# Products with the inverse for both heads at once: all four quadrants of the array, and a second head masked across the partition halves

## The chip, the cores and the metric

The kernel runs on one core of a Trainium2 chip. The metric is the device time in microseconds (us) of one execution. TensorE (PE in the rows) does matrix products, VectorE (DVE) and ScalarE (ACT) the elementwise work, SyncE issues the DMAs.

## The reference

The program is two transformer blocks, one behind the other, on 512 tokens of width 1024. The first block has attention and a convolution; the second has an RWKV-7 time mix of 12 heads of width 64, memory attention and a feed-forward part. The change lies in the time mix, whose core is a recurrence over the tokens:

```python
def step(S, inp):
    r_t, w_t, k_t, v_t, a_t, b_t = inp
    sa = jnp.einsum('bhvk,bhk->bhv', S, a_t)
    S = (S * w_t[:, :, None, :] + sa[..., None] * b_t[:, :, None, :]
         + v_t[..., None] * k_t[:, :, None, :])
    return S, jnp.einsum('bhvk,bhk->bhv', S, r_t)
```

## The kernel before

The recurrence is computed by chunks of C = 64 tokens, eight chunks in 512 tokens, in six pairs of heads (`p` = 0 to 5, two heads `h` each). Within a chunk the state's dependence on itself is a triangular 64 x 64 system. Its matrix must be inverted for each head and chunk: 16 small inverses in a pair. Chunks go by parity `q`: those of one parity stand on partitions 0 to 63, of the other on 64 to 127 (`rows(half)`), and `c` = 0 to 3 counts the chunks of a parity. So one 128 x 256 tile holds all chunks of one head.

The inverse `X` (kept as `XN`, and its transpose as `XT`) grows by levels `b` = 2, 4, 8, 16, 32 (`LEVELS`). In each level and for each head:

1. TensorE: the product with the inverse, `times_inverse`, eight products of 64 x 64 x 64 into the PSUM bank `y{b}_{p}_{h}`. Each product is two MATMUL rows in the trace (L1310, x32 for both heads). It reads partitions `rows(1 - q)` and writes `rows(q)`, so only two of the array's four quadrants work.
2. VectorE: the mask (L2606), `Y[:, h]` = bank times the table `m{b}`. It frees the bank.
3. TensorE: `inverse_update` (L1323 and L1326, x64 for both heads), `Y` with `XT` and `XT` with `Y`, in all four quadrants. In the last level this is `last_update` (L1336, two quadrants, x32).
4. VectorE: the addition (L2641) into `XX`, which holds `XN` and `XT`.

Before, head 0's product waits for head 0's addition of the level before only, and head 1's for head 1's; the mask of head 0 can run while head 1's product does.

Each engine runs its instructions in the order in which they are written; semaphores (`is_full`, `is_free` of a bank) join them. Between these steps stands other work of the same engines. In a middle pair (1, 2, 3) TensorE has: the two halves of the next pair's `v` projection (L857 to L859) before and behind the update of level 4, `gate_low_rank` (L867) at level 8, `masked_values` (L1349) behind level 8, a sum (L1237, L1238) before the update of level 16 and another behind it, and `low_rank` (L867) at level 32 before the last update. VectorE has at level 8 the input of `v` (L2067; it waits for ScalarE's copy of the projection, L1841) ahead of the masks, and L2064 and L2481 between masks and additions; at level 16 L2539 ahead of the masks, L2510 between and L2521, L2493 behind the additions; at level 32 L2527. Pair 0 has no sum and no gate product, since there is no earlier pair. Pair 4 has no `low_rank`. Pair 5 has memory attention (L867, L1024, L1210; L2218 on VectorE) between its steps. Behind the levels come the products for the state chain, the chain itself, and the next pair.

Of the kernel before, what the change touches and what calls it, by code (L numbers as in the profile page):

```python
# [42 lines left out]
ALU = mybir.AluOpType  # L43
# [18 lines left out]
C = 64  # L62
NC = S // C
G = 4
PARITIES = 2
HEADS = 2
# [16 lines left out]
STEPS = NQ * QT  # L83
MTILES = S // P
MUNITS = 2 * MTILES
MU_AMID, MU_BEHIND = {0: 0, 1: 2, 2: 3, 4: 5}, {0: 1, 3: 4}
MU_SOLVE = len(MU_AMID) + len(MU_BEHIND)
MU_CHAIN = MU_SOLVE + 1
# [331 lines left out]
def build(nc, small, tables, xT, ctxT, memT, weights, saved, outT):  # L420
    plan = psum_plan()
    with ExitStack() as ctx:
# [89 lines left out]
        half = at  # L512
# [5 lines left out]
        NT, Y, TK, TV, MAK, MRK = (region(at + i * S, NC, C) for i in range(6)); at += 6 * S  # L518
# [8 lines left out]
        XT, XN = (heads_first(XX[:, i, :].rearrange("p (n t) -> p n t", t=C)) for i in range(2))  # L527
# [66 lines left out]
        def mask(name, *times):  # L594
            m = tab(name)
            for _ in times:
                m = m[:, None]
            return m.to_broadcast([P, *times, C])

        def rows(half):  # L600
            return slice(half * DH, (half + 1) * DH)
# [74 lines left out]
        def bank(name, w=None, rows=slice(0, P)):  # L676
            b, n = plan[name][:2]
            return psum[rows, b * S:b * S + (w or n * S)]
# [33 lines left out]
        def full_inc(ins, name):  # L712
            ins.then_inc(full[plan[name][0]], 1)

        def free_inc(ins, name):
            ins.then_inc(free[plan[name][0]], 1)
# [96 lines left out]
        def _(pe):  # L813
# [87 lines left out]
            outs = {}  # L901
# [393 lines left out]
            def key_products(name, p, x):  # L1295
                take(name)
                out = by_head(name)
                for c in range(G):
                    for q, h in QH:
                        ins = pe.matmul(out[rows(q), h, c], x[rows(h), 2 * c + q, :],  # L1300
                                        AR[p % 2][rows(h), :, 2 * c + q, :], start=True, stop=True)
                        if c == G - 1:
                            full_inc(ins, name)

            def times_inverse(name, h):

                out = take(name, G * C).rearrange("p (c t) -> p c t", c=G)
                for c in range(G):
                    for q in range(PARITIES):
                        ins = pe.matmul(out[rows(q), c, :], NT[rows(1 - q), h, c, :], XN[rows(1 - q), h, c, :],  # L1310
                                        start=True, stop=True)
                        if c == G - 1:
                            full_inc(ins, name)
# [104 lines left out]
            for p in range(NP):  # L1418
# [14 lines left out]
                for b in LEVELS:  # L1433
                    for h in range(HEADS):
                        if prev is None:
                            pe.wait_ge(x_first, p + 1)
                        else:
                            pe.wait_ge(*is_free(f"x{prev}_{p}_{h}"))
                        times_inverse(f"y{b}_{p}_{h}", h)

                    if p == NP - 1:
                        if b == LEVELS[0]:
                            gn_mean(p - 1)
                        if b == LEVELS[1]:
                            gn_square(p - 1)
                        if b == LEVELS[3]:
                            gate_low_rank(p - 1)
                        memory_unit(MU_AMID.get(LEVELS.index(b)))
                        if b == LEVELS[2]:
                            masked_values(p)  # L1450
                    else:
                        if b == LEVELS[1]:
                            project_part(f"v_{p + 1}", 0, DK // 2)
                        if p and b == LEVELS[2]:
                            gate_low_rank(p - 1)
                        if p and b == LEVELS[3]:
                            gn_square(p - 1)
                        if b == LEVELS[-1] and p + 2 < NP:
                            low_rank(p + 2)
                    for h in range(HEADS):  # L1460

                        pe.wait_ge(*is_free(f"y{b}_{p}_{h}"))
                        if b != LEVELS[-1]:
                            inverse_update(f"x{b}_{p}_{h}", h)
                        else:

                            last_update(f"xf_{p}_{h}", h)
                    if p == NP - 1:
                        memory_unit(MU_BEHIND.get(LEVELS.index(b)))
                    else:  # L1470
                        if p and b == LEVELS[0]:
                            gn_mean(p - 1)
                        if b == LEVELS[1]:
                            project_part(f"v_{p + 1}", DK // 2, DK)
                        if b == LEVELS[2]:
                            masked_values(p)
                        if b == LEVELS[3]:
                            bonus_sum(p + 1)
                        if b == LEVELS[-1]:
                            project_part(beside_chain(p, "k"), 0, 2)  # L1480
                    prev = b
# [572 lines left out]
        def _(vec):  # L2054
# [530 lines left out]
            for p in range(NP):  # L2585
# [14 lines left out]
                for b in LEVELS:  # L2600
                    if p + 1 < NP and b == LEVELS[2]:
                        pair_input(p + 1, "v")
                    for h in range(HEADS):
                        name = f"y{b}_{p}_{h}"
                        vec.wait_ge(*is_full(name))
                        free_inc(vec.tensor_tensor(Y[:, h], bank(name, G * C).rearrange("p (c t) -> p c t", c=G),  # L2606
                                                   mask(f"m{b}", G), ALU.mult), name)

                    if p == NP - 1 and b == LEVELS[0]:
                        gn_centre(p - 1)  # L2610
# [315 lines left out]
```

## Time and profile before

| | |
|---|---|
| median of 3 runs | 1069.5 us (1069.06 to 1071.4) |
| profiled execution | 1070.18 us, span 1068.4 us |
| TensorE busy | 1039.6 us, 97% |
| VectorE busy | 653.9 us, 61% |
| ScalarE busy | 453.0 us, 42% |
| granted TensorE clock | 1.0 (mean of the execution) |
| chain that ended last | TensorE 76%, VectorE 16%, ScalarE 4% |

The span is the time from the first to the last record of the profiled execution; its own time is 1.8 us longer. The chain is followed back from the last instruction to what released each one, so its shares say which engine set the time; a busy share alone does not.

### The profile page before, as it was taken

What the parts mean: (1) busy time and instruction counts of PE and PEld (TensorE: products, weight loads), DVE (VectorE), ACT (ScalarE), POOL (GpSimd) and SP (SyncE); (2) the same over time, 40 slices, a digit from 0 to 9 for tenths busy, and PEclk for the clock granted to TensorE, in tenths of its full rate; (3) what the DMA queues carried; (4) which work ended last, traced back from release to release, by engine and by line L of the source; (5) the groups of instructions that cost most, each with busy time, mean ns of one, the idle gap of its engine ahead of it and who ended that gap; (6) DMA issues with size and microseconds to landing.
All of it is one profiled execution on the core that took longest, in us unless ns stands there. A gap on an engine that the chain in (4) does not pass through costs nothing.

```text
span 1068.4 us, 22579 instructions
## 1 busy us (share of the span) xinstructions
PE 1039.6 (97%) x9816; PEld 823.4 (77%) x9816; DVE 653.9 (61%) x1025; ACT 453.0 (42%) x732; POOL 5.6 (1%) x10
## 2 busy tenths in 40 slices
PE   7999999999999989999999999999999999999998
PEld 5777777676777777777777767787888888888887
DVE  4569999977466665868677667664443223444322
ACT  5455555686335533443535245344432112443111
POOL 0000000000000000000000000000000000000000
PEclk9999999999999999999999999999999999999999
DMA  9912224000532110110110121322222232223230
GB/s 360 377 61 99 79 81 176 1 2 2 197 118 79 60 42 22 43 42 25 39 42 22 42 81 43 124 93 99 99 99 99 99 99 88 93 96 114 89 104 30
DMA packets 26161, 95.01 MB, mean 89 GB/s; under 512 B 2896, under 2 KB 3152, under 8 KB 25552
## 3 DMA queue, kind: packets, MB, share of 16 engines
q1 hardware_dynamic: 26064, 93.57, 25.1%
q8 instruction: 79, 1.29, 0.5%
q14 instruction: 18, 0.15, 0.0%
HBM read 89.36 MB, written 4.19 MB: 88 GB/s over the span
## 4 chain that ended last, share of the span: by engine, by line
PE 76%; DVE 16%; ACT 4%; issue 2%; DMA 1%; SPq 1%; POOL 0%; ACTq 0%; DVEq 0%
PE psum L857 19%; PE psum L858 18%; PE psum L859 18%; DVE work L2067 5%; PE psum L867 3%; PE psum L1310 2%; PE psum L1323 2%; DVE small_temps L2218 1%; PE psum L1045 1%; PE psum L1024 1%; PE psum L1359 1%; PE psum L1382 1%; DMA work<-weights 1%; DVE in_weights_low L2123 1%; PE psum L1110 1%
## 5 line engine op out<-in xcount | busy, mean ns | idle before, releaser
L2123 DVE TENSOR_TENSOR weights_low<-ring,weights_high 128x1024 fp32r<-128x1024 f32 x70 | 85.8, 1226 | 75.3 <-ACT weights_high L1673 75.3
L1673 ACT ACTIVATE weights_high<-ring 128x1024 fp32r<-128x1024 f32 x70 | 73.6, 1052 | 127.5 <-PE psum L859 127.5
L857 PE MATMUL psum<-normed_high,weights_high 128*128 128x512 f32 x256 | 100.2, 391 | 0.2 <-DVE weights_low L2123 0.2
L859 PE MATMUL psum<-normed_high,weights_low 128*128 128x512 f32 x256 | 99.7, 389 | 0.0
L859 PE MATMUL psum<-hidden_high,weights_low 128*128 128x512 f32 x256 | 99.7, 389 | 0.0
L858 PE MATMUL psum<-normed_low,weights_high 128*128 128x512 f32 x256 | 99.6, 389 | 0.0
L858 PE MATMUL psum<-hidden_low,weights_high 128*128 128x512 f32 x256 | 99.6, 389 | 0.0
L857 PE MATMUL psum<-hidden_high,weights_high 128*128 128x512 f32 x256 | 99.6, 389 | 0.0
L2067 DVE SCALAR_TENSOR_TENSOR work<-work,small_sb 128x512 f32<-128x512 f32 x116 | 80.2, 745 | 0.2
L1643 ACT ACTIVATE work<-psum 128x384 f32<-128x384 f32 (+1 forms) x110 | 54.1, 541 | 56.3 <-PE psum L1359 18.8
L857 PE MATMUL psum<-pair_normed_high,pair_weights_high 128*128 128x512 f32 x176 | 75.8, 431 | 0.8 <-DVE normed_low L2127 0.8
L858 PE MATMUL psum<-normed_low,pair_weights_high 128*128 128x512 f32 x176 | 69.3, 394 | 0.0
L859 PE MATMUL psum<-pair_normed_high,pair_weights_low 128*128 128x512 f32 x176 | 68.9, 392 | 0.0
L2046 ACT ACTIVATE work<-work 128x512 f32<-128x512 f32 x32 | 20.2, 632 | 100.9 <-DVE work L2064 100.9
L857 PE MATMUL psum<-normed_high,in_weights_high 128*128 128x512 f32 x144 | 59.2, 411 | 1.9 <-DVE in_weights_low L2123 1.6
L857 PEld LDWEIGHTS psum<-normed_high,weights_high 128*128 128x128 f32 x256 | 48.1, 188 | 10.8 <-issue 0.9
L859 PE MATMUL psum<-normed_high,in_weights_low 128*128 128x512 f32 x144 | 56.2, 390 | 0.0
L858 PE MATMUL psum<-normed_low,in_weights_high 128*128 128x512 f32 x144 | 56.2, 390 | 0.0
L859 PEld LDWEIGHTS psum<-normed_high,weights_low 128*128 128x128 f32 x256 | 48.1, 188 | 10.1
L858 PEld LDWEIGHTS psum<-normed_low,weights_high 128*128 128x128 f32 x256 | 48.1, 188 | 10.1 <-issue 0.2
L859 PEld LDWEIGHTS psum<-hidden_high,weights_low 128*128 128x128 f32 x256 | 48.1, 188 | 10.0
L857 PEld LDWEIGHTS psum<-hidden_high,weights_high 128*128 128x128 f32 x256 | 48.1, 188 | 9.9
(320 smaller groups left out, 2102.6 us busy)
## 6 DMA issues: line engine op xcount, KB each, us to landing
ring<-weights SPq DMA_DIRECT2D x135, 512.0 KB, 3.7
work<-weights SPq DMA_DIRECT2D x10, 512.0 KB, 12.9
residual<-xT SPq DMA_DIRECT2D x4, 512.0 KB, 7.1
mixed<-weights SPq DMA_DIRECT2D x4, 512.0 KB, 7.8
residual_saved<-residual SPq DMA_DIRECT2D x8, 256.0 KB, 4.4
residual<-residual_saved SPq DMA_DIRECT2D x1, 2048.0 KB, 9.0
outT<-residual SPq DMA_DIRECT2D x8, 256.0 KB, 3.3
tables_sb<-tables SPq DMA_DIRECT2D x1, 1280.0 KB, 10.4
```

The lines of the kernel that those rows point to most:

```text
L857: pe.matmul(out, wh, high(k), start=first and n == 0, stop=False)
L858: pe.matmul(out, wh, low(k), start=False, stop=False)
L859: ins = pe.matmul(out, wl, high(k), start=False, stop=last and n == len(order) - 1)
L867: full_inc(pe.matmul(take(name, w), stationary, moving, start=True, stop=True), name)
L1024: last = pe.transpose(out[:, t * P:(t + 1) * P], src[:, t * P:(t + 1) * P], tab("ident"))
L1310: ins = pe.matmul(out[rows(q), c, :], NT[rows(1 - q), h, c, :], XN[rows(1 - q), h, c, :], start=True, stop=True)
L1323: ins = pe.matmul(out[rows(q), 0, c, :], Y[rows(q), h, c, :], XT[rows(q), h, c, :], start=True, stop=True)
L1643: free_inc(act.activation(out, bank(name, w) if src is None else src, ACT.Copy), name)
L1673: act.activation(wsplit(q)[0], room_of(b), ACT.Copy).then_inc(w_high, 1)
L2046: act.activation(FS[:, t, :], FS[:, t, :], ACT.Square).then_inc(h_relu, 1)
L2067: return vec.scalar_tensor_tensor(out=out, in0=a, scalar=scalar, in1=b, op0=op, op1=ALU.add)
L2123: vec.tensor_tensor(low, room_of(b), high.bitcast(F32), ALU.subtract).then_inc(w_low, 1)
```

## The change

`times_inverse_both` replaces the two calls of `times_inverse` at the levels 4, 8, 16 and 32 (`CROSSED`); level 2 stays. It interleaves the heads and sends head 1's products to the other half of the partitions (`rows(q ^ h)`), so that four products in a row lie in four quadrants. Both heads' banks are taken and both additions waited for before the first product. Head 1's result then stands in the bank with its halves exchanged; so its mask is two instructions over 64 partitions each, which read one half and write the other.

```diff
+CROSSED = (4, 8, 16, 32)
...
+            def times_inverse_both(p, b):
+
+                names = [f"y{b}_{p}_{h}" for h in range(HEADS)]
+                outs = [take(name, G * C).rearrange("p (c t) -> p c t", c=G) for name in names]
+                for c in range(G):
+                    for q in range(PARITIES):
+                        for h in range(HEADS):
+                            ins = pe.matmul(outs[h][rows(q ^ h), c, :], NT[rows(1 - q), h, c, :],
+                                            XN[rows(1 - q), h, c, :], start=True, stop=True)
+                            if c == G - 1:
+                                full_inc(ins, names[h])
+
...
                             pe.wait_ge(*is_free(f"x{prev}_{p}_{h}"))
-                        times_inverse(f"y{b}_{p}_{h}", h)
+                        if b not in CROSSED:
+                            times_inverse(f"y{b}_{p}_{h}", h)
+                    if b in CROSSED:
+                        times_inverse_both(p, b)
...
-                        free_inc(vec.tensor_tensor(Y[:, h], bank(name, G * C).rearrange("p (c t) -> p c t", c=G),
-                                                   mask(f"m{b}", G), ALU.mult), name)
+                        y, m = bank(name, G * C).rearrange("p (c t) -> p c t", c=G), mask(f"m{b}", G)
+                        if h == 0 or b not in CROSSED:
+                            ins = vec.tensor_tensor(Y[:, h], y, m, ALU.mult)
+                        else:
+                            for half in range(2):
+                                ins = vec.tensor_tensor(Y[rows(half), h], y[rows(1 - half)], m[rows(1 - half)], ALU.mult)
+                        free_inc(ins, name)
```

On TensorE, at level 16 of pair 2, the program before has two groups of eight products with a wait each (`psum_free0` and `psum_free2` are the additions and masks that free banks; a product is one row here and two in the trace):

```order
L1349 MATMUL psum<-work 64x64 x15
L1310 MATMUL psum<-work 64x64 [waits psum_free2]
L1310 MATMUL psum<-work 64x64 x7
L1310 MATMUL psum<-work 64x64 [waits psum_free2,psum_free0]
L1310 MATMUL psum<-work 64x64 x7
L1237 MATMUL psum<-norm_high,heads_rounded 128x512 [waits heads_rounded,psum_free5,gn_squares]
```

and after the change one group of sixteen, which waits for both (lines are shifted by the new code: 1310 is 1313, 1349 is 1362, 1237 is 1238):

```order
L1362 MATMUL psum<-work 64x64 x15
L1313 MATMUL psum<-work 64x64 [waits psum_free2,psum_free0]
L1313 MATMUL psum<-work 64x64 x15
L1238 MATMUL psum<-norm_high,heads_rounded 128x512 [waits heads_rounded,psum_free5,gn_squares]
```

The second wait has moved ahead of head 0's products; nothing else on this engine changed its place.

On VectorE, levels 8 and 16 of pair 2, before (2606 are masks, 2641 additions):

```order
L2067 SCALAR_TENSOR_TENSOR work<-psum,small_sb,work 128x511
L2606 TENSOR_TENSOR work<-psum,tables_sb 128x256 x2
L2064 SCALAR_TENSOR_TENSOR work<-work,small_sb,head_rstd 128x512
L2481 TENSOR_TENSOR bonus_low<-t_t_61,bonus_high 128x512
L2641 TENSOR_TENSOR work<-psum,work 128x2x16x8 x2
L2539 TENSOR_TENSOR norm_squares_low<-head_squares,norm_high 128x512
L2606 TENSOR_TENSOR work<-psum,tables_sb 128x256 x2
L2510 SCALAR_TENSOR_TENSOR work<-work,t_t_61 128x512
```

and after (2624 is the full mask, 2627 the two halves):

```order
L2083 SCALAR_TENSOR_TENSOR work<-psum,small_sb,work 128x511
L2624 TENSOR_TENSOR work<-psum,tables_sb 128x256
L2627 TENSOR_TENSOR work<-psum,tables_sb 64x256 x2
L2080 SCALAR_TENSOR_TENSOR work<-work,small_sb,head_rstd 128x512
L2497 TENSOR_TENSOR bonus_low<-t_t_61,bonus_high 128x512
L2662 TENSOR_TENSOR work<-psum,work 128x2x16x8 x2
L2555 TENSOR_TENSOR norm_squares_low<-head_squares,norm_high 128x512
L2624 TENSOR_TENSOR work<-psum,tables_sb 128x256
L2627 TENSOR_TENSOR work<-psum,tables_sb 64x256 x2
L2526 SCALAR_TENSOR_TENSOR work<-work,t_t_61 128x512
```

The second mask of a level is two instructions instead of one; there are 24 more VectorE instructions in the program.

## Rows read from the trace of the kernel before

**Rows 1.** The page: span, and busy time of TensorE and VectorE

```profile
span 1068.4 us, 22579 instructions
...
PE 1039.6 (97%) x9816; PEld 823.4 (77%) x9816; DVE 653.9 (61%) x1025; ACT 453.0 (42%) x732; POOL 5.6 (1%) x10
```

**Rows 2.** Busy time of the engines in the levels of pair 2

```profile
482.40:504.60 22.20, 22.11 (x519) 17.22 (x517) 17.89 (x36) 9.27 (x16) 0.00 (x0) 1.00 0.09 27
```

**Rows 3.** The chain of waits, pair 2: start, us, what

```profile
495.81 0.20 PE psum L1323
...
496.90 0.93 PE psum L1349 x32
...
501.24 1.08 PE psum L1310 x32
502.31 1.21 PE psum L867 x4
```

**Rows 4.** Timeline of VectorE, pair 2: start, us, what, idle time before

```profile
494.52 0.75 DVE L2067 SCALAR_TENSOR_TENSOR work<-psum,small_sb,work 128x511 f32<-128x511 f32 x1 [1.41 <-ACT work L1841]
495.18 0.74 DVE L2606 TENSOR_TENSOR work<-psum,tables_sb 128x256 f32<-128x256 f32 x2
...
497.11 0.75 DVE L2641 TENSOR_TENSOR work<-psum,work 128x256 f32<-128x256 f32 x2
...
498.40 0.89 DVE L2606 TENSOR_TENSOR work<-psum,tables_sb 128x256 f32<-128x256 f32 x2
...
500.25 0.89 DVE L2641 TENSOR_TENSOR work<-psum,work 128x256 f32<-128x256 f32 x2 [0.37 <-PE psum L1326]
...
502.26 0.75 DVE L2606 TENSOR_TENSOR work<-psum,tables_sb 128x256 f32<-128x256 f32 x2
```

**Rows 5.** Timeline of TensorE, pair 2, where products and updates start

```profile
495.74 0.27 PE L1323 MATMUL psum<-work 64*64 64x64 f32 x1
...
497.67 1.15 PE L1310 MATMUL psum<-work 64*64 64x64 f32 x32
...
499.41 0.27 PE L1323 MATMUL psum<-work 64*64 64x64 f32 x1
...
503.45 1.15 PE L1336 MATMUL psum<-work 64*64 64x64 f32 x32
```

**Rows 6.** Timeline of VectorE: instructions over 64 and over 128 partitions

```profile
336.65 0.41 DVE L2074 TENSOR_SCALAR sigmoids<-sigmoids 64x512 f32<-64x512 f32 x1
337.10 0.42 DVE L2415 COPY work<-t_t 64x512 f32<-64x512 f32 x1
...
369.93 0.76 DVE L2074 TENSOR_SCALAR sigmoids<-sigmoids 128x512 f32<-128x512 f32 x2
```

**Rows 7.** Timeline of TensorE, pairs 0 and 4, where it waits for VectorE

```profile
389.30 0.70 PE L1310 MATMUL psum<-work 64*64 64x64 f32 x17 [0.16 <-DVE work L2641]
...
399.45 0.27 PE L1323 MATMUL psum<-work 64*64 64x64 f32 x1 [0.90 <-DVE work L2606]
...
598.45 1.15 PE L1336 MATMUL psum<-work 64*64 64x64 f32 x32 [0.42 <-DVE work L2606]
```

**Rows 8.** Timeline of VectorE, pairs 0 and 4

```profile
400.91 0.75 DVE L2641 TENSOR_TENSOR work<-psum,work 128x256 f32<-128x256 f32 x2
402.20 0.89 DVE L2606 TENSOR_TENSOR work<-psum,tables_sb 128x256 f32<-128x256 f32 x2 [0.54 <-PE psum L1310]
...
597.98 0.75 DVE L2606 TENSOR_TENSOR work<-psum,tables_sb 128x256 f32<-128x256 f32 x2
```

**Rows 9.** Timeline of VectorE, pair 5, level 16: masks and additions

```profile
644.73 0.75 DVE L2606 TENSOR_TENSOR work<-psum,tables_sb 128x256 f32<-128x256 f32 x2
646.04 0.89 DVE L2641 TENSOR_TENSOR work<-psum,work 128x256 f32<-128x256 f32 x2 [0.56 <-PE psum L1326]
```

**Rows 10.** Timeline of VectorE, pair 2, behind the levels

```profile
510.86 0.69 DVE L2677 TENSOR_TENSOR work<-psum,tables_sb 128x512 f32<-128x512 f32 x1 [1.98 <-PE psum L1370]
```

## The prediction

> **What bounds the kernel now.** I read the page first: TensorE is busy for 97% of a span of 1068.4 us, VectorE for 61% [rows 1]. The profiled execution took 1070.18 us, 0.68 above the median of the timed runs (1069.5), so there is some 1.8 us around the span, and I sum against 1070.2. The change touches only the inversion levels of the six pairs of heads, from about 386 to 653 us. So next I asked for the busy time of one such stretch, the levels of pair 2 (482.4 to 504.6): TensorE 22.11 of 22.20 us, VectorE 17.89 [rows 2]. That looks like a stage bound by TensorE alone, where anything cut from TensorE is gain. The chain of waits and VectorE's timeline correct this. The chain runs over TensorE all the time [rows 3], but from 494.52 to the masks of level 32 at 502.26 VectorE has nearly no idle time either: 0.37 us, before the row at 500.25 [rows 4]. The two engines hand the work to each other there, and both are full. Only before 494.52 has VectorE room (1.41 us idle).
>
> **What the change takes from TensorE.** At levels 4 to 32 a product with the inverse is 32 MATMUL rows of 64x64 and holds TensorE for 1.08 us (501.24, [rows 3]), 34 ns each. It uses two quadrants. The update behind it has 64 such rows in all four quadrants and holds TensorE from 495.81 to 496.90, 1.09 us, so 17 ns each [rows 3]. I price the new product by that row: 32 x 17 ns = 0.54 us. It saves 0.54 us at each of 24 places, 13 us in all if nothing waited. A bound from the other side is no saving (34 ns each, as now).
>
> **What it adds to VectorE.** The second head's mask becomes two instructions over 64 partitions and the same 256 columns. One mask takes 0.42 us; two back to back 0.75 us, so the second starts 0.33 after the first [rows 4]. Does half the partitions halve the time? The trace has TENSOR_SCALAR over 64x512 in 0.41 us and over 128x512 twice in 0.76, 0.42 each [rows 6]: no, columns set it. How far apart do they start? The ordinary row overlaps its neighbour by 0.09. But the COPY at 337.10, which follows a TENSOR_SCALAR without a wait and works on the other partition half, starts 0.03 us after the end of that one (336.65 + 0.41 = 337.06) instead of 0.09 before it [rows 6]. The new halves read one half and write the other, so they, and the full-width instruction behind them, change halves each time. I take steps of 0.45 us (0.42 + 0.03), as that COPY is the nearest row. Three steps of 0.45 instead of two of 0.33: VectorE gets 0.69 us more per level, 16.6 us in 24 places; the second head's masked product is ready 1.32 us after its level's first mask starts, where it was 0.75. With the ordinary step it would be 0.33 and 1.08 us.
>
> The Trainium skill, VectorE: DVE Perf Modes, section "Two Vector instructions with no wait between them", has the rule: an instruction whose start quadrant differs from the last one read or written in that memory is held until every earlier Vector instruction has finished. The trace agrees in that one COPY. By the rule the steps are the held ones, by the plain neighbours they are 0.33; both sums are below.
>
> **What moves.** Both heads' products now wait for both heads' additions, and the first mask waits for (nearly) the whole joint product instead of half of two.
>
> **Middle pairs (1, 2, 3), by the times of pair 2.** Level 4: nothing waits, the product ends 0.54 earlier, VectorE's 0.69 goes into its idle 1.41. Level 8: the v projection ends 0.54 earlier, so the v input starts at 493.98 and the mask of head 0 at 494.64 (was 495.18). An update starts 0.06 us after its mask's end (mask 597.98 + 0.42, update 598.45 [rows 7, 8]), so head 1's can start at 494.64 + 1.32 + 0.06 = 496.02 (was 495.74 + 0.54 = 496.28 [rows 5]). VectorE behind it is 0.69 - 0.54 = 0.15 late, and its additions end at 498.01 (497.11 + 0.75 before [rows 4]). Level 16: the joint product starts 0.15 us after that (as in pair 0 at 389.30, 0.16 idle behind the addition [rows 7]), at 498.16, where head 0's started at 497.67 [rows 5], and ends at 498.70, as before. But the first mask (498.40 before) comes at 498.81: it used to run during head 1's product. Head 1's update moves to 500.19 (was 499.41 + 0.54 [rows 5]), the additions end at 501.51 (was 501.14); the idle 0.37 has absorbed part. Level 32: product from 501.66 to 502.20 (was to 502.24); the low-rank product of 1.2 us (502.31, [rows 3]) hides the mask of head 0, at 502.26 + 0.37 = 502.63; head 1's last update comes at 502.63 + 1.32 + 0.06 = 504.01 against 503.45 + 0.54 = 503.99 [rows 5]. So the pair ends where it did: 0.0 us. Behind it VectorE has 1.98 us idle before it is needed again [rows 10].
>
> **Pair 0.** TensorE here already waits for head 0's addition at level 4 (389.30): start 0.54 later, 0.54 shorter, nothing gained. At level 8 it waits 0.90 us for the first mask [rows 7], whose time is set by the v input; VectorE behind is 0.69 late, so the additions end at 400.91 + 0.75 + 0.69 = 402.35 [rows 8], the product runs from 402.50 to 403.04 and the first mask comes at 403.15 (was 402.20 [rows 8]). After its masks VectorE is 1.5 us late (403.15 + 1.35 against 402.20 + 0.89 - 0.09), and so are the additions and the level-32 product's start, minus 0.54: the pair ends **1.0 later**.
>
> **Pair 4.** As a middle pair, but no low-rank product stands before the last update: TensorE waits 0.42 us for the mask [rows 7]. VectorE is 0.37 late there; head 1's mask ends at 597.98 + 0.37 + 1.32 = 599.67 [rows 8], the last update's second half starts at 599.73 (was 598.45 + 0.54): **0.75 later**.
>
> **Pair 5** has memory attention between the levels. Level 4 gives 0.54, level 8 0.07 more (the product waits for both additions, 0.47 more, but is 0.54 shorter). At level 16 VectorE is the later one: masks at 644.73 - 0.61, head 1's update at 644.12 + 1.32 + 0.06 = 645.50 (was 644.73 + 0.42 + 0.06 + 0.54 = 645.75), 0.25 earlier, and the additions, which end at 646.93 now [rows 9], 0.36 earlier; level 32 gives 0.54: **0.9 earlier**.
>
> Sum: 1.0 + 3 x 0.0 + 0.75 - 0.9 = +0.85 us. Behind the levels TensorE works through the projections and products of the state chain, and then through the feed-forward part, without slack, so that goes to the end: 1071.0 for the profiled run, **1070.3** against the median.
>
> **Rivals.**
> - *VectorE's halves overlap as usual* (step 0.33). For it: every full-width neighbour; only one row speaks against it. Worked in the same way: middle pairs 0.76 earlier each (additions of level 8 end at 497.65, level 16 product from 497.80, level 32 product ends at 501.48), pair 0 0.3 later, pair 4 0.2 earlier, pair 5 1.2 earlier: -3.4 us, 1066.1. Chance 0.22.
> - *Each change of half costs more* (the other side: slower). The COPY reads SBUF in a fast form (512 columns in 0.42 us), the masks read PSUM and a table, 256 columns in 0.42. If start waits 0.10 us after an end instead of 0.03, eight such starts on each pair's path (three at level 8, three at 16, two at 32) add 8 x 0.07 = 0.56 us: 2.8 over five pairs, with pair 5 counted as half 3.1 at most: 1073.2. It counts as slower from a gap of about 0.06 us. Chance 0.23.
> - *The product doesn't get faster*: 34 ns a row remains. Then the joint start costs and nothing pays: about 1.5 us in each middle pair, 2.7 and 2.0 in pairs 0 and 4: near +10, 1080. The update row speaks against it: it too has both row halves writing in one bank. Chance 0.04. The Trainium skill, TensorEngine Tiling (Array Packing), "Restrictions and Gotchas", would favour this rival: different row tiles must not access the same PSUM bank at the same time. The trace disagrees where it can be seen: the update at 17 ns does just that.
>
> The forecast itself has 0.51.
>
> **Range.** Two of the cases beside the forecast lie within 4.3 us; 1066 to 1073.3 takes in the first two rivals. The likeliest case alone: 1069.3 to 1071.8 (gap 0.01 to 0.05). 0.2% is 2.1 us, about what a measurement can tell from no change: faster 0.26 (first rival and a little of the forecast's edge), same 0.47, slower 0.27 (second and third).
>
> **What the changed profile would show.** The joint product's 32 rows in 0.54 us; the half masks 0.42 us each, starts 0.45 apart, and the next VectorE row 0.03 after their end; TensorE waiting for the second head's mask at levels 8 and 16 with idle times near 0.35 us; the span between the first level's start and the last update in pairs 1 to 3 unchanged at 22.1 us, in pair 0 longer by 1. The prediction is wrong if the halves start 0.33 apart (then TensorE hardly waits), or if a VectorE row lasts longer than 0.42 across halves. If the joint product's rows come 34 ns apart the third rival holds.

## The result and the profile after the change

The change makes the kernel slower by less than half a per cent: 1073.93 us (median of 6 runs, 1072.84 to 1075.57) against 1070.36 us for the kernel before in the same rounds (6 runs, 1067.41 to 1072.1). The ratio is 1.0037, with a 95% interval of 1.002 to 1.0054. The profiled execution took 1074.34 us. The forecast was 1070.3 with a range up to 1073.3: too low by 3.6 us, and outside its range.

The page of the kernel after, span and busy times:

```profile
span 1072.6 us, 22603 instructions
...
PE 1035.3 (97%) x9816; PEld 815.8 (76%) x9816; DVE 664.9 (62%) x1049; ACT 453.0 (42%) x732; POOL 5.6 (1%) x10
```

Against [rows 1] TensorE is busy 4.3 us less and VectorE 11.0 us more, and the span is 4.2 us longer. TensorE lost work and gained idle time. The page's group of the half masks (x count, then busy us and mean ns of one, then idle us before them) and that of the joint product:

```profile
L2627 DVE TENSOR_TENSOR work<-psum,tables_sb 64x256 f32<-64x256 f32 x48 | 20.3, 422 | 1.1
...
L1313 PE MATMUL psum<-work 64*64 64x64 f32 x768 | 16.7, 224 | 3.9 <-DVE work L2662 3.9
```

A half over 64 partitions takes the 0.42 us of a full mask. The joint product waits for VectorE's additions (L2662) for 3.9 us in all.

Pair 2, the same stretch as [rows 2] (it begins 1.2 us later here, since the pairs before are longer), by the windows: length, then busy us of TensorE, weight loads, VectorE, ScalarE, GpSimd, clock, DMA share, GB/s:

```profile
483.60:506.40 22.80, 21.40 (x519) 15.80 (x517) 20.61 (x42) 9.30 (x15) 0.00 (x0) 1.00 0.08 26
```

TensorE has 1.40 us of it idle, where it had 0.09. VectorE is busy for 20.61 of 22.80 us; it was 17.89 of 22.20. TensorE, which ran through these levels, now stops for VectorE. VectorE's timeline shows how, start and duration first ([rows 4] are the same places before):

```profile
495.36 0.75 DVE L2083 SCALAR_TENSOR_TENSOR work<-psum,small_sb,work 128x511 f32<-128x511 f32 x1 [0.69 <-ACT work L1857]
496.02 0.41 DVE L2624 TENSOR_TENSOR work<-psum,tables_sb 128x256 f32<-128x256 f32 x1
496.47 0.86 DVE L2627 TENSOR_TENSOR work<-psum,tables_sb 64x256 f32<-64x256 f32 x2
497.36 0.75 DVE L2080 SCALAR_TENSOR_TENSOR work<-work,small_sb,head_rstd 128x512 f32<-128x512 f32 x1
...
498.63 0.75 DVE L2662 TENSOR_TENSOR work<-psum,work 128x256 f32<-128x256 f32 x2
...
500.25 0.42 DVE L2624 TENSOR_TENSOR work<-psum,tables_sb 128x256 f32<-128x256 f32 x1 [0.27 <-PE psum L1313]
500.70 0.86 DVE L2627 TENSOR_TENSOR work<-psum,tables_sb 64x256 f32<-64x256 f32 x2
...
503.46 0.68 DVE L2509 TENSOR_TENSOR work<-psum,work 128x512 f32<-128x512 f32 x1
504.06 0.41 DVE L2624 TENSOR_TENSOR work<-psum,tables_sb 128x256 f32<-128x256 f32 x1
504.50 0.86 DVE L2627 TENSOR_TENSOR work<-psum,tables_sb 64x256 f32<-64x256 f32 x2
```

From the full mask at 496.02 to the first half is 0.45 us; the two halves take 0.86; the row behind them starts at 497.36, 0.03 behind their end at 497.33. VectorE pays one start gap behind the full mask, one between the halves and one behind them, three steps of 0.44 to 0.46 us. TensorE in the same pair (in the changed kernel L1336 and L1339 are the update, L1349 is the last update and L1362 `masked_values`):

```profile
496.49 0.27 PE L1336 MATMUL psum<-work 64*64 64x64 f32 x1 [0.29 <-DVE work L2624]
...
497.47 0.24 PE L1336 MATMUL psum<-work 64*64 64x64 f32 x1 [0.28 <-DVE work L2627]
...
503.05 0.69 PE L1313 MATMUL psum<-work 64*64 64x64 f32 x32
503.67 1.65 PE L868 MATMUL psum<-work,small_sb 64*128 64x512 f32 x4
505.25 1.15 PE L1349 MATMUL psum<-work 64*64 64x64 f32 x32
```

The first head's update starts at 496.49, 0.06 us behind its full mask (496.02 + 0.41), the second head's at 497.47, 0.14 us behind the halves' end. Between the two starts lie 0.98 us. Read from the starts of TensorE's rows in the same way, this distance is 0.94 to 0.98 us at levels 8 and 16 of pairs 0 to 4 and at level 16 of pair 5, and 0.52 us where nothing is waited for, as before the change. So at these eleven places the wait takes back 0.42 to 0.46 us, all or nearly all of the 0.46 that the joint product has saved. The joint product holds TensorE for 0.62 us (503.05 to 503.67). The low-rank product behind it (L868) lasts from 503.67 to 505.25, 1.58 us where it was 1.21 [rows 3]. The chain of waits at level 16 and 32 of pair 2 (start, us, what) runs over VectorE at level 16:

```profile
500.32 0.38 issue
500.70 0.42 DVE work L2627
501.14 0.43 DVE work L2627
501.57 0.14 issue
...
503.06 0.68 PE psum L1313 x32
503.74 1.58 PE psum L868 x3
505.32 1.08 PE psum L1349 x32
```

What decides is how long a pair takes. This table is worked out from the starts of TensorE's rows in each trace: the time in us from the first product of a pair's levels to the first product that uses its finished inverse (`solve`, L1359 before and L1372 after; in pairs 0 to 4 six rows of a projection stand between the last update and it), and the sum over the pairs. The runs named e1 to e12 are those of the next section.

```
pair        0      1      2      3      4      5      sum
before  22.79  23.68  23.65  24.10  22.95  26.02   143.19
after   24.24  24.46  24.26  24.33  23.96  26.64   147.89
e1      23.07  23.12  23.14  23.14  22.43  25.14   140.04
e2      23.64  23.98  23.69  23.76  23.18  25.73   143.98
e3      23.98  24.44  24.42  24.44  24.01  26.65   147.94
e4      23.95  24.06  24.06  24.08  23.56  26.98   146.69
e5      22.83  23.33  23.55  23.25  22.58  25.56   141.10
e6      22.76  23.31  23.25  23.32  22.60  25.44   140.68
e7      24.20  24.29  24.28  24.30  23.98  26.01   147.06
e8      24.18  24.92  24.63  24.64  23.90  27.21   149.48
e9      22.78  23.31  23.25  23.38  22.88  25.44   141.04
e10     22.65  23.50  23.52  23.67  23.35  26.01   142.70
e11     24.24  24.31  24.31  24.38  24.34  25.92   147.50
e12     24.25  24.29  24.24  24.28  23.98  26.65   147.69
```

Pair 3 of before holds a stray stall of 0.43 us (a gap put down to "issue" between two halves of a product at 546.18); without it it takes 23.67, as its neighbours. Pair 2 of e5 holds one of the same kind (TensorE's rows stop for 0.37 us within a product, at 499.84); without it it takes 23.18. No other entry of the table holds one. The change adds 4.70 us to the sum (5.13 without the stall of before), 4.2 to the span; outside the pairs the two traces differ by small gaps of both signs, the largest 1.17 us of "issue" at 478.36 of before only. e12 is the changed kernel again: its row of the table agrees with the first run to 0.2 us in any pair.

### The profile page after: what moved, and what is told of

Read it like the earlier page. It is cut to its first block, busy times and chain, and to the rows that moved or that the text cites. A ratio compares the mean times of both kernels' runs of the same rounds, so it can differ in the third digit from the quotient of the medians.

```text
span 1072.6 us, 22603 instructions
## 1 busy us (share of the span) xinstructions
PE 1035.3 (97%) x9816; PEld 815.8 (76%) x9816; DVE 664.9 (62%) x1049; ACT 453.0 (42%) x732; POOL 5.6 (1%) x10
## 4 chain that ended last, share of the span: by engine, by line
PE 71%; DVE 19%; ACT 4%; issue 3%; DMA 1%; SPq 1%; POOL 0%; ACTq 0%; DVEq 0%
PE psum L858 19%; PE psum L859 18%; PE psum L860 18%; DVE work L2083 6%; PE psum L868 2%; DVE small_temps L2234 2%; DMA ring<-weights 1%; PE psum L1046 1%; PE psum L1336 1%; PE psum L1025 1%; PE psum L1313 1%; PE psum L1395 1%; PE psum L1372 1%; DVE work L2627 1%; DVE work L2080 1%
```

## The experiments

All ratios are of the time of the run against the kernel before, on the same chip, with 95% intervals. The edits are shown shortened: indentation is left out, and with a choice by pair the tests `b in CROSSED` become `(p, b) in CROSSED`.

**One and two full masks, all else as after (e1, e2).** Both kernels leave head 1's halves exchanged, so these measure time only.

```diff
# e1                                   # e2
-for half in range(2):                 -for half in range(2):
-    ins = vec.tensor_tensor(Y[rows(half), h], y[rows(1 - half)], m[rows(1 - half)], ALU.mult)
+ins = vec.tensor_tensor(Y[:, h], y, m, ALU.mult)
# e2 has this line behind it:
+ins = vec.tensor_tensor(FB[:, 0:G, :], y, m, ALU.mult)
```

> The changed kernel, but head 1's mask is one full-width instruction again (its halves stay exchanged, so the inverse of head 1 is not the right one; the times do not hang on the values). The joint product in four quadrants stays. If VectorE's two half masks are what costs (theory A), VectorE is back at 0.33 us from mask to mask, the product's saving comes through, and the kernel is 4 to 6 us faster than before (about 1.2 us in a middle pair, 0.8 in pair 4, little in pair 0, 1.5 in pair 5). If the joint start of both heads is what costs (theory B), most of the loss stays: slower than before by 1 us or more. If the product itself does not pay, no change to before.

> The changed kernel, but head 1's mask is two instructions of full width over 128 partitions and 256 columns (the second writes a copy to a buffer that is free then; the halves stay exchanged, so the result is not the right one). The number and length of VectorE's instructions are those of the changed kernel, only no instruction changes halves. Theory A with held starts (0.45 us from start to start when the half changes, 0.33 otherwise): 2 to 4 us faster than before, and some 0.36 us per place, 3 to 5 us in all on the path, faster than the changed kernel. Theory C (the extra instruction is the whole cost, changes of half cost nothing): as the changed kernel, 3 to 4 us slower than before. B: slower than before too.

Measured: e1 1066.4 us, ratio 0.9976 [0.9967, 0.9985]; e2 1069.63 us, 1.0002 [0.9993, 1.0011]. Both came out slower than expected: e1 is 3.1 us faster than before and not 4 to 6, and e2 is level with before and not 2 to 4 us faster, since the third instruction was taken as nearly free. VectorE's timeline of e2 at level 8 of pair 2:

```profile
493.81 0.41 DVE L2624 TENSOR_TENSOR work<-psum,tables_sb 128x256 f32<-128x256 f32 x1
494.14 0.41 DVE L2626 TENSOR_TENSOR work<-psum,tables_sb 128x256 f32<-128x256 f32 x1
494.47 0.42 DVE L2627 TENSOR_TENSOR work<-psum,tables_sb 128x256 f32<-128x256 f32 x1
494.80 0.74 DVE L2080 SCALAR_TENSOR_TENSOR work<-work,small_sb,head_rstd 128x512 f32<-128x512 f32 x1
```

Three masks, all of them full width, start 0.33 us apart, and so does the row behind them: 0.99 us from the first mask to that row, where the halves need 1.34 (496.02 to 497.36 above). The third instruction alone costs 3.9 us in the sum of the pairs (3.2 by the medians), the changes of half another 3.9 (the ratio goes from 1.0002 to 1.0037, 3.7 us). VectorE gets 24 x 0.33 = 7.9 us by the first and 24 x 0.35 = 8.4 us by the second; about half of either reaches the end. The way is seen on TensorE: at the eleven places named above the second head's update starts 0.52 us behind the first head's in e1 (once 0.58), 0.71 to 0.76 in e2, and 0.94 to 0.98 in after.

**Halves alone, no joint product (e3).**

```diff
-ins = vec.tensor_tensor(Y[:, h], y, m, ALU.mult)             # head 1, levels 4 to 32, kernel before
+for half in range(2):
+    ins = vec.tensor_tensor(Y[rows(half), h], y[rows(half)], m[rows(half)], ALU.mult)
```

> The kernel before, with its two separate products, and head 1's mask at levels 4 to 32 as two instructions over 64 partitions, each reading and writing its own half (nothing crosses; the result is right). Only VectorE gets the 0.69 us per place. Theory A: 3.5 to 5 us slower than before, as much as the changed kernel or more, since no product is shorter (0.5 us in a middle pair, about 1.0 in pairs 0 and 4). Steps of 0.45 us although no half is crossed within an instruction. Theory B: no slower than 1 us. If crossing within one instruction, and not the change from one to the next, is what holds it, steps of 0.33 us and at most 2 us slower.

Measured: 1074.35 us, ratio 1.0047 [1.0035, 1.0059], as expected. VectorE's timeline of e3 at the same place:

```profile
496.50 0.42 DVE L2608 TENSOR_TENSOR work<-psum,tables_sb 128x256 f32<-128x256 f32 x1
496.83 0.85 DVE L2611 TENSOR_TENSOR work<-psum,tables_sb 64x256 f32<-64x256 f32 x2
497.71 0.75 DVE L2064 SCALAR_TENSOR_TENSOR work<-work,small_sb,head_rstd 128x512 f32<-128x512 f32 x1
```

Here the halves don't cross: the first reads and writes partitions 0 to 63, as the full mask before it begins there too. It starts 0.33 us behind the full mask, the ordinary step. Only the second half, which begins at partition 64, and the full-width row behind it are held: 0.85 for the two, then 0.03 behind their end at 497.68. In the changed kernel the first half is held as well (0.45), as it reads partitions 64 to 127. That is what the rule named in the prediction says of a change of start quadrant (the Trainium skill, VectorE: DVE Perf Modes, section "Two Vector instructions with no wait between them"); the rule's own condition, a change of quadrant and not the smaller number of partitions, is what tells these two kernels apart. The split costs 4.75 us in the pairs' sum with nothing gained on TensorE.

**The joint start alone (e4).** Both heads' waits and the order of the joint product, but two quadrants as before and full masks.

```diff
-ins = pe.matmul(outs[h][rows(q ^ h), c, :], ...
+ins = pe.matmul(outs[h][rows(q), c, :], ...
...
-for half in range(2):
-    ins = vec.tensor_tensor(Y[rows(half), h], y[rows(1 - half)], m[rows(1 - half)], ALU.mult)
+ins = vec.tensor_tensor(Y[:, h], y, m, ALU.mult)
```

> The kernel before with both heads' products joined in one group, which waits for both additions, but in the two quadrants of before (34 ns a row, 1.08 us for 32 rows), and one full mask for each head (the result is right). It measures the joint start alone. Theory A: 1.5 to 3 us slower than before: 1.2 in pair 0, 0.1 in middle pairs, 0.4 in pair 4. Theory B: 4 us slower or more, so that the four quadrants hide part of it in the changed kernel.

Measured: 1073.42 us, ratio 1.0033 [1.0021, 1.0045], the pairs' sum +3.50 (3.93 without the stall of before). That is more than the 1.5 to 3 us expected, with 0.4 us in each middle pair instead of 0.1. To wait for both additions, and to have the first mask wait for the whole of both products, costs this much by itself. e1 is e4 with four quadrants in place of two: 6.65 us less in the sum, 7.0 in the medians, 6.1 by the ratios. So the change splits into four steps, each between two kernels that were run:

```
sum over the pairs, us
before                                         143.19
e4     both heads joined, two quadrants        146.69   +3.50
e1     four quadrants                          140.04   -6.65
e2     a third mask instruction                143.98   +3.94
after  its two halves change partitions        147.89   +3.91
                                                        +4.70
```

**By level (e5, e8).**

```diff
-CROSSED = (4, 8, 16, 32)
+CROSSED = (4,)            # e5
+CROSSED = (8, 16)         # e8
```

> The change at level 4 alone (the other levels as before; the result is right). There VectorE has over 1 us to spare ahead of the next level and TensorE has the v projection behind both steps. If the change pays where VectorE has room, 0.35 us in each of pairs 1 to 4 (product 0.46 shorter, start 0.08 later), nothing in pairs 0 and 5: 1 to 1.8 us faster than before. If the joint start or the half masks cost as such, wherever they stand: no gain or slower.

> The change at levels 8 and 16 alone (the result is right), where VectorE is full and the update stands close behind the masks. If that is where the loss lies, it is as slow as the whole change or slower: 4 to 6 us above before, 0.8 to 1.0 in each middle pair, since levels 4 and 32 no longer give anything back. If the loss were spread evenly over the levels: 2 us.

Measured: e5 1068.49 us, ratio 0.9986 [0.9976, 0.9996]; e8 1076.8 us, 1.0065 [1.005, 1.0081]. With the two stalls taken out, level 4 gains 0.35 to 0.47 us in each of pairs 1 to 5, also in pair 5, where nothing was expected, and nothing in pair 0, where TensorE already waited there [rows 7]. Levels 8 and 16 alone cost more than the whole change: 6.3 us in the sum, 7.2 in the medians (4 to 6 expected), and 1.06 in a middle pair. The loss sits where VectorE has no room.

**A choice of places (e6).** Level 4 in pairs 1 to 5, level 32 in pairs 0 to 3 and 5, and the rest as before.

```diff
-CROSSED = (4, 8, 16, 32)
+CROSSED = {(p, 4) for p in (1, 2, 3, 4, 5)} | {(p, 32) for p in (0, 1, 2, 3, 5)}
```

> The change at level 4 of pairs 1 to 5 and at level 32 of pairs 0 to 3 and 5: the places where, by the traces, TensorE has work between product and update that hides the half masks (projection, low-rank product, memory attention); everything else as before, the result is right. Expected where the room decides: 0.3 us in pair 0, 0.65 in each of pairs 1 to 3, 0.35 in pair 4, 0.4 in pair 5: 3.0 us faster than before, between 2 and 3.5. If level 32 does not pay, as level 4 alone, 1 to 1.8 us.

Measured: 1067.38 us, ratio 0.9979 [0.9969, 0.9989]: faster than both kernels, by 2.2 us against before, at the low end of what was expected. In the pairs nearly all of it is level 4: against e5, without its stall, level 32 adds 0.12 in pair 5, 0.07 in pair 0 and nothing on average over pairs 1 to 3 (23.29 against 23.25). By the medians e6 is 1.1 us ahead of e5, but the intervals of the two overlap.

**Pair 5 without its level 8 (e7).** The pair that was forecast to gain most had lost. The trace of after shows what it waits for, in its timeline (in order of time; idle time before a row and its releaser in brackets):

```profile
641.99 0.42 DVE L2624 TENSOR_TENSOR work<-psum,tables_sb 128x256 f32<-128x256 f32 x1 [0.87 <-PE psum L1313]
642.45 0.86 DVE L2627 TENSOR_TENSOR work<-psum,tables_sb 64x256 f32<-64x256 f32 x2
643.33 0.75 DVE L2234 TENSOR_REDUCE small_temps<-psum 128x1 f32<-128x256 f32 x2
...
643.85 0.47 ACT L1778 ACTIVATE work<-psum,small_temps 128x256 f32<-128x256 f32 x1 [3.08 <-DVE small_temps L2234]
...
644.56 0.45 PE L1362 MATMUL psum<-work 64*64 64x64 f32 x8 [0.84 <-ACT work L1778]
```

The row maxima of memory attention (L2234) stand on VectorE behind the masks of level 8. ScalarE's exponentials (L1778) wait for them, and TensorE's `masked_values` (L1362 here, L1349 before) come behind the products of memory attention, which wait for the exponentials: 0.84 us idle, where TensorE was idle for under 0.1 us before. e7 leaves this one place as before.

```diff
-CROSSED = (4, 8, 16, 32)
+CROSSED = {(p, b) for p in range(6) for b in (4, 8, 16, 32)} - {(5, 8)}
```

> The changed kernel, but level 8 of pair 5 as before (the result is right). In the changed kernel TensorE waits 0.8 us there for ScalarE's exponentials, which wait for a row maximum that stands behind the half masks on VectorE. If that is the chain: pair 5, from its first product to the solve, 0.5 to 0.8 us shorter than in the changed kernel (26.64 us there), and the time that much lower, 3 us above before. If the memory attention is late for another reason, pair 5 stays at 26.6 us.

Measured: 1074.82 us, ratio 1.0049 [1.0033, 1.0065]; 3 us above before were expected, 5.2 were measured. Against 1.0037 of the changed kernel this is inside the intervals, so the times don't show the gain. Pair 5 does: 26.01 against 26.64, and the other pairs agree to 0.04 us except pair 1 (0.17). VectorE's timeline of e7:

```profile
640.24 0.89 DVE L2624 TENSOR_TENSOR work<-psum,tables_sb 128x256 f32<-128x256 f32 x2 [0.41 <-PE psum L1323]
641.33 0.76 DVE L2234 TENSOR_REDUCE small_temps<-psum 128x1 f32<-128x256 f32 x2 [0.20 <-PE psum L868]
```

The maxima start 1.09 us behind the first mask; in the changed kernel it is 1.34 (641.99 to 643.33), and the mask itself comes later, since it waits for the joint product.

**The low-rank product's bank (e9, e10).** In pair 2 L868 takes 1.58 us at level 32 of the changed kernel instead of 1.21. Its second product (two of the four rows) writes a bank that VectorE's L2509 (the bonus product) has to free, and L2509 now comes at 503.46 and ends at 504.14; the second product starts at 504.20. The groups of waits before L868 in the levels of pairs 0 to 4 (us, times), in the changed kernel:

```profile
  DVE tables_sb L2509: 0.5, 2
  DVE work L2509: 0.5, 2
```

e10 is the kernel before with `bonus` ahead of `scaled_b` on VectorE; e9 is e6 with the same exchange.

```diff
-scaled_b(p + 1)
 bonus(p + 1)
+scaled_b(p + 1)
```

> The control: the kernel before with nothing but the exchange of the bonus product and the scaled B on VectorE (the result is right). TensorE does not wait for that bank there, so no change: within 0.1%, pairs 1 to 3 at 23.7 us.

> The chosen places (level 4 of pairs 1 to 5, level 32 of pairs 0 to 3 and 5), and on VectorE behind level 16 the bonus product ahead of the scaled B instead of behind it (the result is right). At level 32 the second low-rank product on TensorE waits 0.2 to 0.5 us for the bank that the bonus product frees, and so the saving of the joint product is lost. Freed 0.3 us earlier, pairs 1 to 3 should end 0.2 to 0.4 us earlier than with the chosen places alone (23.25 to 23.32 us there from first product to solve), 3 us faster than before in all. If another wait stands behind that one, the pairs stay at 23.3 us.

Measured: e10 1069.44 us, ratio 0.9999 [0.999, 1.0009]; e9 1068.98 us, 0.999 [0.9981, 0.9999]. So the exchange gives nothing to either: e9 is no better than e6 and rather worse (pair 4 +0.28, the others within 0.06), where 3 us faster than before had been expected and 1.0 was measured. In e10 pair 4 is 0.40 longer too, and pairs 0 to 2 are 0.13 to 0.18 shorter. The wait did go. TensorE's timeline of e6 at level 32 of pair 1:

```profile
451.12 0.69 PE L1313 MATMUL psum<-work 64*64 64x64 f32 x32
451.75 1.65 PE L868 MATMUL psum<-work,small_sb 64*128 64x512 f32 x4
453.33 1.15 PE L1349 MATMUL psum<-work 64*64 64x64 f32 x32
```

and of e9:

```profile
451.68 0.69 PE L1313 MATMUL psum<-work 64*64 64x64 f32 x32
452.31 1.34 PE L868 MATMUL psum<-work,small_sb 64*128 64x512 f32 x4
453.58 1.45 PE L1349 MATMUL psum<-work 64*64 64x64 f32 x32
```

The low-rank product takes 1.27 instead of 1.58 us up to the next start. The last update takes 0.30 longer: it now waits for VectorE's masks, which are no earlier than they were. The time moved from one wait to the next, with VectorE behind both.

**Both waits out of the changed kernel (e11), and the changed kernel beside it (e12, no edit).**

```diff
-CROSSED = (4, 8, 16, 32)
+CROSSED = {(p, b) for p in range(6) for b in (4, 8, 16, 32)} - {(5, 8)}
...
-scaled_b(p + 1)
 bonus(p + 1)
+scaled_b(p + 1)
```

> The changed kernel without the two waits that the prediction had not named: level 8 of pair 5 as before, and the bonus product ahead of the scaled B on VectorE, so that the low-rank product's bank at level 32 is free earlier (the result is right). If these two waits are the error of the prediction and not the price of a change of half: pairs 0 to 3 some 0.2 to 0.35 us shorter than in the changed kernel (24.24, 24.46, 24.26, 24.33 us from first product to solve), pair 5 at 26.0 instead of 26.6 us, and 1.2 to 2 us faster than the changed kernel in all. If behind the low-rank product another wait takes over at once, as with the chosen places, only pair 5's 0.6 us.

> The changed kernel itself, once more, for a comparison on the same chip: 3 to 4.5 us slower than before, ratio 1.003 to 1.0045.

Measured: e11 1073.6 us, ratio 1.0038 [1.0025, 1.0051]; e12 1074.06 us, 1.0041 [1.0029, 1.0053]. Against e12 pair 5 is 0.73 better, pair 4 is 0.36 worse, pairs 1 to 3 stay within 0.1; as a whole the two are level, where 1.2 to 2 us had been expected or, with another wait behind, 0.6. What the last update (L1349) waits for in the levels of pairs 0 to 4 of the changed kernel (us, times):

```profile
  DVE work L2624: 4.7, 6
  DVE work L2627: 0.5, 2
```

and in e11:

```profile
  DVE work L2624: 5.4, 6
  DVE work L2627: 1.4, 6
```

The 1.0 us that L868 no longer waits for L2509 is back as 1.6 us more for the masks. The bank's wait is real, but it isn't what the time hangs on; VectorE's sequence is.

## Why the prediction was wrong

**What held.** The 48 half masks take 0.42 us each. The gap behind an instruction of the other half is 0.03 us, the steps 0.44 to 0.46, as taken from the one COPY row [rows 6]. The first rival (halves overlap, 1066.1) fell by these rows, and e2 shows what it would have been about: with three overlapping masks the time is that of before, not 3.4 us better. The third rival (34 ns a row) fell too: 32 rows in 0.62 us are 19 ns each. The second rival forecast the size (up to 1073.2), but not by its mechanism: the gap didn't grow to 0.10. (Its own terms, 1070.3 + 3.1, make 1073.4; the measured time lies above that too.) From the first mask to the row behind the halves it is 1.34 us (496.02 to 497.36), where 1.35 was forecast. So the prices on VectorE were right; what they do on the path was not.

**The steps that failed.** By its own pair terms the prediction had +0.85, measured +4.70, an error of 3.85 (0.43 more without the stall of before).

*"The low-rank product of 1.2 us ... hides the mask of head 0 ... So the pair ends where it did: 0.0 us"* (pairs 1 to 3; error 1.6 us). Measured +0.78, +0.61 and +0.23 (0.66 without the stall of before). In pair 2, with times from its first product, forecast and measured:

```
                                     forecast   measured
joint product, level 16, starts         15.70      15.83
joint product, level 32, starts         19.20      19.40
low-rank product starts                 19.74      20.02
last update starts                      20.95      21.60
its second half can start               21.55      21.85
```

The forecasts are the prediction's own times less 482.46 (the last update's start, which it doesn't state, is the product's end at 502.20 plus the 1.21 of [rows 3]); the last row measured is the half masks' end at 505.36 plus 0.14 less 483.65. Three small terms were each too low: the joint product takes 0.62 us, not 0.54 (503.05 to 503.67); the second head's update starts 0.14 behind its mask's end (497.33 to 497.47), not 0.06; and level 4's joint product waits for both additions, 0.08 later. The largest single one, 0.37 us (1.58 against 1.21), is the wait of L868 for the bank of L2509, and no term of the prediction had it: VectorE's L2509 stood between additions and masks in the order of the engines, and the working followed only the masks. That the cover itself could wait for the engine that it covers is the step that was left out. e9 and e11 then showed that with this wait gone the time is the same: the second half of the last update waits for the half masks, which are 0.3 us late too. That pair 0 came out 1.45 (forecast 1.0) and pair 4 1.01 (0.75) fits the same small terms, but wasn't taken apart.

*"Pair 5 ... 0.9 earlier"* (error 1.5 us). The runs give each level's share, each from two kernels that differ in it alone. Forecast increments are from the prediction's text: 0.54 and 0.07 earlier, then from 0.61 to 0.36, then 0.54.

```
pair 5          forecast   measured
level 4            -0.54      -0.46   before to e5
level 32           -0.54      -0.12   e5 to e6
level 16           +0.25      +0.57   e6 to e7
level 8            -0.07      +0.63   e7 to after
sum                -0.90      +0.62
```

Level 8's failed step is shown: the chain masks, row maxima, exponentials, products was not followed; the prediction counted only the masks' way to the update. Levels 16 and 32 were mis-sized, 0.3 and 0.4 us, and no run separates their waits, but the traces show where the time goes. At level 32 the rows at `solve` of e5, then of e6, are:

```profile
650.19 1.05 PE L1372 MATMUL psum<-work 64*64 64x128 f32 x15 [0.16 <-issue]
650.01 1.20 PE L1372 MATMUL psum<-work 64*64 64x128 f32 x18 [0.50 <-DVE work L2662]
```

The joint product saves 0.45 us up to the last update; 0.34 of it is lost where TensorE waits for VectorE's last additions (L2662), which in e6 come without a gap behind the half masks and the instructions of memory attention; in e5 VectorE had been idle for 0.35 us before them. Again it is what is queued behind the halves. At level 16 the rows of e7 are:

```profile
645.29 0.69 PE L1313 MATMUL psum<-work 64*64 64x64 f32 x32 [0.66 <-DVE work L2662]
...
648.00 0.24 PE L1336 MATMUL psum<-work 64*64 64x64 f32 x1 [0.29 <-DVE work L2627]
```

The joint product waits for both additions, 0.66 us where e6 waits 0.23 for one, which takes back its saving. The second head's update starts 1.45 us behind the first mask (646.55), where e6 has 0.98: 0.47 us later. And its rows last 0.72 us where e6 has 0.58; the forecast had nothing for that. Why a second half that was waited for lasts longer was not tried.

The same splitting works in the middle pairs, as a mean over pairs 1 to 3 with both stalls taken out (before 23.67, e5 23.25, e6 23.29, after 24.35, e8 24.73): level 4 gives -0.42, level 32 +0.04, levels 8 and 16 +1.06, and e8, which has these two alone, stands at +1.06 as well. So the levels add up, and the loss is that of levels 8 and 16, where the prediction expected the idle 0.37 us [rows 4] and the earlier v input to pay for them.

**What the prediction weighed wrongly.** It found both engines full from 494.52 on, and yet took each of VectorE's microseconds as hidden whenever the next event on TensorE had been late before. The ladder above shows the exchange: of 11 us taken from TensorE (24 x 0.46) 6.65 reach the end, of the 16.3 that VectorE gets 7.85, and the joint start takes 3.5 to 3.9. Its sign for the sum of these was right, by little; its size was not.

## What to carry to other kernels

Where two engines hand work to each other and both are near full, a change that takes 1 from one and gives 1.5 to the other is not free: look for the stretches in which the receiving engine has idle time and make the change only there, as e5 did (level 4, where VectorE has 1.41 us idle in a middle pair). A place picked because the other engine has work to cover it, as e6 did with level 32, gave next to nothing. Before a stall is called hidden behind some product, ask what that product itself waits for; and follow every instruction queued behind the lengthened one, not only the one that the change is about. To join two streams has its own price, which can be measured alone (e4), and it was more than half of what the four quadrants gave.

## What the runs showed of the hardware

- A VectorE instruction that begins in another partition half than the one before starts 0.03 us behind its end instead of 0.09 before it (497.36 of after, 497.71 of e3), also where it reads PSUM (496.47 of after); a straight first half after a full-width mask isn't held (496.83 of e3).
- Half the partitions don't shorten an instruction: 64x256 takes 0.422 us, as 128x256 does.
- Rows of 64x64 products in four quadrants come 19 to 20 ns apart (32 rows in 0.62 us), with both row halves writing in one bank, against 34 ns in two quadrants [rows 3] and 17 ns in the update. Why the joint product is slower than the update was not tried.
- TensorE, idle for it, starts 0.06 us behind the end of the first head's full mask (496.43 to 496.49), 0.14 behind that of the second head's halves (497.33 to 497.47), and 0.10 behind the additions of level 8 (499.38 to 499.48). Why they differ was not tried.
